# Gathered rows added two blocks sooner in a value stage, and the second norm's first block normalised at once

## What is computed

```python
def peer_ffn(x, w_q, sub_keys, u, v):        # per chunk of 128 tokens
    ...                                       # top 16 experts of each of 8 heads, gates = softmax
    ue = jnp.take(u, experts, axis=0)
    ve = jnp.take(v, experts, axis=0)
    act = jax.nn.gelu(jnp.einsum('chkd,cd->chk', ue, xc), approximate=False)
    return jnp.einsum('chk,chkd->cd', gates.astype(xc.dtype) * act, ve)
...
for l in range(DEPTH):
    h = x @ w_in[l]                           # three kinds of attention, w_o
    ...
    x = layer_norm(DEEPNORM_ALPHA * x + mix, ln1_g[l], ln1_b[l])
    ffn = peer_ffn(x, peer_w_q[l], peer_sub_keys[l], peer_u[l], peer_v[l])
    x = layer_norm(DEEPNORM_ALPHA * x + ffn, ln2_g[l], ln2_b[l])
```

## Time and profile before

| | us |
|---|---|
| median of 3 runs | 3308.46 (3307.1 to 3309.74) |
| the profiled execution | 3310.66 |
| its span, first to last instruction | 3308.8 |
| TensorE (PE) busy | 3209.9 (97%) |
| VectorE (DVE) busy | 2544.9 (77%) |
| GpSimd (POOL) busy | 1955.6 (59%) |
| ScalarE (ACT) busy | 1298.3 (39%) |
| mean granted TensorE clock, share of full | 0.991 |
| value stage, layer 0 | about 1120 to 1643 |
| value stage, layer 1 | about 2765 to 3288 |

### The profile page before, as it was taken

One profiled execution on the slowest core, in us unless ns is written; L12 is line 12 of the kernel. 1 busy time (PEld: TensorE's weight loads), 2 busy tenths in 40 slices (PEclk: granted clock), 3 DMA queues, 4 the chain that ended last, 5 costly groups with the idle time before them and its releaser, 6 DMA issues. The chain is left out here.

```text
span 3308.8 us, 64646 instructions
## 1 busy us (share of the span) xinstructions
PE 3209.9 (97%) x18502; PEld 2948.2 (89%) x18502; DVE 2544.9 (77%) x5455; ACT 1298.3 (39%) x2054; POOL 1955.6 (59%) x1556
## 2 busy tenths in 40 slices
PE   8999999999999999999899999999999999999997
PEld 8898889999999888888798988899999998888886
DVE  1466567888888899999924655588888888999998
ACT  2355234444444333333324542344444443333332
POOL 3445338888654466666544443488886544666665
PEclk9999999999999999999999999999999999999999
DMA  4002139999787799999820011399997877999996
GB/s 168 28 1 77 39 90 303 321 321 307 249 299 249 262 337 335 338 338 332 280 96 25 1 77 51 101 315 320 321 314 247 292 253 265 339 339 336 337 331 216
DMA packets 249399, 765.14 MB, mean 231 GB/s; under 512 B 28384, under 2 KB 95712, under 8 KB 241376
## 3 DMA queue, kind: packets, MB, share of 16 engines
q1 hardware_dynamic: 170400, 459.95, 41.9%
q0 software_dynamic: 73728, 268.47, 21.6%
q10 hardware_dynamic: 5184, 35.65, 3.0%
HBM read 677.98 MB, written 85.98 MB: 231 GB/s over the span
## 5 line engine op out<-in xcount | busy, mean ns | idle before, releaser
L685 POOL TENSOR_TENSOR st_lo<-st_raw,st_hi 128x1024 fp32r<-128x1024 f32 x290 | 697.7, 2406 | 463.4 <-ACT st_hi L947 458.4
L947 ACT CAST st_hi<-st_raw 128x1024 fp32r<-128x1024 f32 x544 | 569.7, 1047 | 659.7 <-PE ps L1975 659.7
L1892 PE MATMUL ps<-t_hi,st_hi 128*128 128x384 f32 (+1 forms) x2288 | 794.6, 347 | 1.4 <-ACT st_hi L947 1.3
L1893 PE MATMUL ps<-t_lo,st_hi 128*128 128x384 f32 (+1 forms) x2288 | 786.8, 344 | 0.0
L793 POOL TENSOR_TENSOR wt_lo<-w_f,wt_hi 128x384 fp32r<-128x384 f32 x256 | 416.7, 1628 | 318.6 <-ACT wt_hi L1073 318.5
L1896 PE MATMUL ps<-t_hi,st_lo 128*128 128x384 f32 (+1 forms) x2288 | 462.3, 344 | 0.3
L1892 PEld LDWEIGHTS ps<-t_hi,st_hi 128*128 128x128 f32 x2288 | 430.2, 188 | 12.2 <-ACT st_hi L947 2.3
L1893 PEld LDWEIGHTS ps<-t_lo,st_hi 128*128 128x128 f32 x2288 | 430.1, 188 | 10.2
L1896 PEld LDWEIGHTS ps<-t_hi,st_lo 128*128 128x128 f32 x2288 | 408.3, 188 | 11.7 <-POOL st_lo L685 1.1
L990 ACT ACTIVATE h_out<-ps 128x384 f32<-128x384 f32 x256 | 125.7, 491 | 697.3 <-PE ps L1896 601.5
L1975 PE MATMUL ps<-st_hi,wt_hi 128*128 128x512 f32 x1536 | 390.0, 389 | 1.4 <-ACT wt_hi L1073 1.4
(11 more groups left out here) (218 smaller groups left out, 5097.7 us busy)
## 6 DMA issues: line engine op xcount, KB each, us to landing
st_raw<-in_peer_u SPq DMA_DIRECT2D x256, 512.0 KB, 4.2
st_raw<-in_peer_v SPq DMA_DIRECT2D x256, 512.0 KB, 4.8
gelu_d<-h_out SPq DMA_DIRECT2D x256, 192.0 KB, 5.3
h_in<-gelu_d SPq DMA_DIRECT2D x256, 192.0 KB, 5.5
gates_d<-g_stage ACTq DMA_DIRECT2D x32, 1024.0 KB, 6.0
g_ch<-gates_d SPq DMA_DIRECT2D x56, 512.0 KB, 6.2
w_raw<-in_w_in SPq DMA_DIRECT2D x16, 1168.0 KB, 5.2
st_raw<-in_peer_w_q SPq DMA_DIRECT2D x32, 512.0 KB, 3.6
```

The source lines that it names most:

```text
L685: nc.gpsimd.tensor_tensor(st_lo[:, s].rearrange("p c f -> p (c f)"), st_raw[:, r], st_hi[:, s].rearrange("p c f -> p (c f)").bitcast(F32), ...
L947: nc.scalar.copy(st_hi[:, r % 2].rearrange("p c f -> p (c f)"), st_raw[:, r]).then_inc(st_h, 1)
L1892: nc.tensor.matmul(dst, st_hi[:, s, c], t_hi[:, c, rows], start=c == 0, stop=False)
L1893: nc.tensor.matmul(dst, st_hi[:, s, c], t_lo[:, c, rows], start=False, stop=False)
```

## The change

Four things are changed. VectorE adds row b + 2 and not row b in its step for block b, from block 4 on; the first four steps add rows 0 to 3 as before, and rows 4 and 5 follow at once, with the loops unrolled where that needs it; no addition remains after the last step. GpSimd's queue is reordered to match: before request r stands share r - 3, where share r - 1 stood, so shares 1 to 3 move behind the first requests, and the last three shares come at the end. VectorE normalises token block 0 right after its statistics, makes the statistics of block 1 next, and then, in layer 0, the residue of block 0 before the shift of the tail block; in layer 1 the statistics of block 2 come before that shift. ScalarE's order follows: the weights of the next layer are rounded right after the deviation of block 0, then token block 0, and only then come the deviation and the first part of the tail block.

```diff
--- before.py
+++ after.py
@@ -797,21 +797,21 @@
             numbers_v(0, 0)
             for b in range(VRING):
                 gather_v(0, 0, b, first=True)
-                if b < 2:
-                    share(b, b)
-            share(2, 0)
+                if b == 0:
+                    share(0, 0)
             with pool.Fori(0, EB // 8 - 1) as i:
                 for part in range(2):
                     g = 2 * i + 1 + part
                     numbers_v(g, 1 - part)
                     for k in range(VRING):
-                        share(8 * i + 4 * part + k + 3, 1 - k % 2)
+                        share(8 * i + 4 * part + k + 1, 1 - k % 2)
                         gather_v(g, 1 - part, k)
             numbers_v(EB // 4 - 1, 1)
             for k in range(VRING):
-                share(EB - 5 + k, 1 - k % 2)
+                share(EB - 7 + k, 1 - k % 2)
                 gather_v(EB // 4 - 1, 1, k)
-            share(EB - 1, 1)
+            for b in range(EB - 3, EB):
+                share(b, b % 2)
             if l + 1 < L:
                 rest_first(l + 1)
             norm_tail(1)
@@ -1083,14 +1083,15 @@
                 round_gated(EB - 2 + s, s)
 
             tail = LN_TAIL[1]
-            for tb in range(tail + 1):
-                deviation(2 * l + 1, tb)
+            deviation(2 * l + 1, 0)
             if l + 1 < L:
                 round_first(l + 1)
+                round_tokens(3 * l + 3, 0)
+            deviation(2 * l + 1, 1)
+            if l + 1 == L:
+                deviation(2 * l + 1, 2)
             shifted(2 * l + 1, total_of(tail))
-            if l + 1 < L:
-                round_tokens(3 * l + 3, 0)
-            for tb in range(tail + 1, TB):
+            for tb in range(tail + 1 + (l + 1 == L), TB):
                 deviation(2 * l + 1, tb)
             if l + 1 < L:
                 round_tokens(3 * l + 3, 1)
@@ -1576,13 +1577,13 @@
 
             dve.wait_ge(g_ev, TN // GRP * (l + 1) + RING)
             dve.sem_inc(waited, 1)
-            def two(b, r, slot, ahead=2):
+            def two(b, r, slot, ahead=2, lead=2):
 
                 for k in range(2):
                     rest_value(b + k + 2, (r + k + 2) % RAW)
                     if k < ahead:
                         gated(b + k + 3, 1 - k, g_ch[:, :, ds(slot + k, 1)])
-                    add_row(b + k, r + k)
+                    add_row(b + k + lead, (r + k + lead) % VRING)
 
             def chunk_landed(c, slot):
 
@@ -1594,7 +1595,19 @@
             for b in range(LEAD):
                 gated(b, b % 2, g_3[:, :, b:b + 1])
             per_ch = GCH // VRING
-            with dve.Fori(0, EB // GCH // 2 - 1) as c:
+            chunk_landed(0, 0)
+            two(0, 0, 0, lead=0)
+            two(2, 2, 2, lead=0)
+            for b in range(VRING, VRING + 2):
+                add_row(b, b % VRING)
+            with dve.Fori(1, per_ch) as k:
+                two(4 * k, 0, 4 * k)
+                two(4 * k + 2, 2, 4 * k + 2)
+            chunk_landed(0, 1)
+            with dve.Fori(per_ch, 2 * per_ch) as k:
+                two(4 * k, 0, 4 * k)
+                two(4 * k + 2, 2, 4 * k + 2)
+            with dve.Fori(1, EB // GCH // 2 - 1) as c:
                 for slot in range(2):
                     chunk_landed(c, slot)
                     with dve.Fori(slot * per_ch, (slot + 1) * per_ch) as k:
@@ -1606,9 +1619,6 @@
                     two(EB - 2 * GCH + 4 * k, 0, 4 * k)
                     two(EB - 2 * GCH + 4 * k + 2, 2, 4 * k + 2)
             two(EB - 4, 0, 2 * GCH - 4, 1)
-            for b in range(EB - 2, EB):
-                add_row(b, b % VRING)
-
             step.at(at)
 
             def total_stats(tb):
@@ -1639,11 +1649,14 @@
             dve.wait_ge(s_ln, 16 * (2 * l + 2))
             dve.sem_inc(waited, 1)
             total_stats(0)
+            normalize_total(0)
             total_stats(1)
-            normalize_total(0)
+            next_rest(0)
+            if l + 1 == L:
+                total_stats(2)
             shift(2 * l + 1)
-            total_stats(2)
-            next_rest(0)
+            if l + 1 < L:
+                total_stats(2)
             total_stats(3)
             normalize_total(2)
             next_rest(1)
```

## The result

The changed kernel takes 3313.01 us (median of 18 runs, 3310.73 to 3316.74) against 3308.39 for the kernel before in the same session: 1.0016 times as long, 95% interval 1.001 to 1.0022. It is slower by 4.6 us. That is clear of 1 in the interval, but less than the 0.2% (6.6 us) that I had set as the bound of what such a measurement can tell from no change. A repetition on another occasion, beside the experiments, gave 3313.19 us, 1.0018 (1.0009 to 1.0027). The profiled span grew from 3308.8 to 3312.7 us.

What follows compares the result with a forecast made beforehand. TensorE bounds the value stage, VectorE's additions and norm the chain behind it. Start +8.1, end -1.9, between the layers -2.7 gave +3.5 us, so 3312.0 us was forecast, range 3304.5 to 3318.

Steps and rivals of the forecast that it cites:

- Start of the stage: First blocks of the value stage, both layers: TensorE waits for GpSimd's shares, 8.1 us more (4 to 14).
- the ring: Value stage start: request waits for row addition, share (wt_lo subtraction) for request, TensorE and gating for share, next addition for gating.
- hand-over: Value stage start, from the end of a row's addition to the request waiting for it: 0.15 us.
- tie: Blocks 3 and 4: next subtraction ready 2.98 us after a share, next share starting at 2.99; subtraction first means 1.0 us late.
- Rival 2: Value stage start: every turn held, 6 us instead of 4 to 5; 14 us stall, +9.5 us, 3318; chance 0.23.
- copy of numbers: Block 5, between request 7 and share 5: takes 0.2 us and the wait behind it 0.81.
- End of layer 1: Behind the last subtraction: two additions fewer, VectorE ends 2.4 us sooner, last transfer may wait 0.5; 1.9 us less.
- Between the layers: From layer 0's value stage to the next projection: earlier rounding and residues, 2.7 us less (1.2 to 4.2).
- GpSimd's chain: Between the layers: two weight residues, then two tail-block norm instructions, ending 3.3 us sooner; the projection waits for them.
- The clock: TensorE's granted clock between the layers: falls in the second gap, more work at 1.2 GHz, 0.6 us back.
- that cover: Value stage start: slack after share 5 hides the two moved additions, costed at nothing; without it up to 1 us.
- Whether a request is held: Layer 0, block 2: request 4 held by VectorE's subtraction gives 2.3 us of stall, 1.4 if not held.

Runs made afterwards that it cites:

- share order mended: The changed kernel, but GpSimd's shares run ahead as in the kernel before up to request 7: 3307.57 us, 0.9998 of the kernel before.
- the ring in every block: The kernel before with only GpSimd's changed order of requests and shares, additions not moved forward and norm as before: 3578.31 us in the one run.
- the one-scalar shift: The changed kernel with the tail block's shift as one tensor_scalar, inverse deviation as per-partition scalar: 3312.92 us, 1.0014 of the kernel before.

## Why the prediction was right, and where it was not

**The sum.** Forecast +3.5 us, measured +4.6 between the medians. The sign of each term was right, and each was near enough: start +8.1 forecast, +9.4 by the marks; end -1.9 and -1.8; between the layers -2.7 and -2.1. The marks together give +5.5, 0.9 more than the medians.

**Start of the stage.** Right in mechanism: the waits name the share, there are four a layer, and the experiments take them away (share order mended) and spread them over the stage (the ring in every block). Block 2 cost 1.97 us in layer 0, where I had 2.3, and 1.86 in layer 1, where I had 1.0. Blocks 3 and 4 cost 0.84 us each, so 1.7 for the two where I took 1.5, and block 5 cost 1.0 where I had 0.9.

The step that was wrong is the hand-over from an addition to the request that waits for it. I took 0.15 us, also as a sign to look for. It is 0.81 to 0.83 us for requests 4 to 7 of both layers. I had read it in the earlier trace rows, where a request starts at 1579.08, 0.15 us behind an addition. But counted from the start of the stage this is request 113, and its own row, 109, had been added at 1574.85. It didn't wait for the addition that the bracket names. The right value stands in the earlier trace rows: row 0 is added until 1131.45, and request 4 starts at 1132.26.

This is why I let request 4 of layer 1 go before the subtraction, for a stall of 1.0 us. In the first profile it would have come second in any case: the activations of block 2 came 1.1 us later than in the kernel before, so the subtraction was ready by the time row 0 was added. In the repetition they were as early as before. Row 0 was still 0.6 us later than summed, since share 1, moved back by the change, held the gating of block 2 (1.18 us). With 0.15 us the request would have started at 2774.59, just ahead of the subtraction of 2774.65. It started at 2775.26, and the stall was 1.72 us.

**Where the sum was lucky.** In blocks 3 and 4 the longer hand-over does no harm, since the subtraction was ready 2.83 us after the last share and not 2.98. With 0.15 us the share would have started 2.97 us after the last one, so it would have come second too. What I called a tie wasn't one: the share starts 0.8 us after the subtraction. In block 5 two errors cancel. The hand-over is 0.67 us longer, and the copy of numbers with the wait behind it costs 0.44 us instead of 1.01: a share follows it there, and the 0.81 us that I took are from a row in which a request follows. Rival 2 was nearer than I wrote. Requests 5 and 6 start 0.15 and 0.17 us ahead of the subtraction and not 0.8.

**End of layer 1.** VectorE's last instruction comes 2.4 us sooner, as summed (19.5 to 17.15). The last transfer starts behind two others. From VectorE's end to the span's end it is 3.55 us where it was 2.98, so 0.57 us against the 0.5 of the forecast; the same 3.56 us stand in the kernel with the norm's new order alone.

**Between the layers.** Two steps were off, in opposite directions. GpSimd's chain was to bring the transposes of block 1 3.3 us forward; it was 2.1, since the shift was held by GpSimd's residue. I had applied this hold to subtractions and gatings and not to an instruction of one element a partition, though the trace before had it at 1.36 us. The rule that I quoted from the Trainium skill (SBUF — State Buffer, Who interferes with whom) makes no exception for small instructions, and the runs agree: 1.70 us with two SBUF inputs, 0.21 with one in the same place. With that step mended the transposes of block 1 come after 13.6 us, where I had predicted 17.2 - 3.3 = 13.9. The clock was to cost 0.6 us back: from the transposes of block 1 to those of block 2 it is 6.0 us in both kernels, so the low clock cost nothing more in the changed one; with the one-scalar shift it did (6.8). I had dated the fall in the kernel before at 1647.8 us; by the 0.77 in the earlier trace rows it was 1647.5, which changes nothing.

**What I had ruled out, rightly.** That VectorE's two additions after block 3 would stop TensorE: not in the changed kernel, where TensorE had been stopped already. But that cover is the ring's stall itself; with the ring open they cost 0.9 us a layer. I had named the cover and up to 1 us for its loss.

**Whether a request is held.** The Trainium skill (SBUF — State Buffer, Who interferes with whom) infers that the making of a gather's descriptors is not held up by such a VectorE instruction. The runs don't agree. In the changed kernel request 4 of layer 0 takes 1.17 us and ends 0.85 us after the subtraction that was running when it started; in the repetition that of layer 1 takes 1.47 and ends 0.86 us after it; requests 5 and 6, started just ahead of the subtraction, take 0.96. What part of the request is held no run here shows. The 0.8 us between an addition and its request is another thing, since requests 5 and 6 have it too; what it consists of is open.

## What to carry to other kernels

If work is moved forward in one of several queues that hold each other by semaphores, follow the ring once around at the start, where the lead is not there yet. An order that is free in the steady part can be a closed loop for the first turns, and the time of a turn is set by the slowest way around, not by any engine's load. Let the lead grow one item at a time, and keep the old order until it exists. Take the price of a hand-over from an instruction that really waited for the one before it: count both from the start of the stage, since the releaser named in a bracket can be wrong. And look at the tiny instructions on the path: here one that reads two SBUF tensors waited for GpSimd's subtraction to end, for one element a partition.

## What was not expected of the hardware

- A VectorE instruction on 128x1 took 1.70 us beside GpSimd's subtraction, 0.16 alone, and 0.21 beside it with one of its inputs given as a scalar per partition.
- A request that waits for an addition starts 0.8 us behind its end, while one that finds its row added starts 0.15 to 0.3 us behind the share before it.
- TensorE's granted clock fell to 1.2 GHz in the changed kernel at about 1651.8 us, though the transposes of block 0 (1.07 us of matmuls from 1649.47 on) lay in the gap: this burst didn't keep it up. In the profile of the one-scalar shift it fell inside the value stage, behind the first wait for a share.
